# The first loads on two queues: ScalarE issues columns, constants and x, SyncE begins with the modulation weights

## The chip, the cores and the metric
One core of a Trainium2 chip. The time is that of one launch on the device, in microseconds (us), the median of several runs. The core has five engines that run their own instruction streams and meet at semaphores: TensorE (PE in the profile; PEld is its loading of weights), VectorE (DVE), ScalarE (ACT), GpSimd (POOL) and SyncE (SP), which here does nothing but issue loads and stores. The transfers themselves are done by 16 DMA engines that the core has for all its queues.

## The reference
Batch 1, 256 tokens, width 1024, everything in float32. A first block and then two layers of another kind:

```python
cond = silu(c)
mod = cond @ ada_w + ada_b                     # 1024 x 6144, split in sh1, sc1, g1, sh2, sc2, g2
h = rmsnorm(x, norm1_g) * (1 + sc1) + sh1
z = h @ w_in                                   # 1024 x 2048: xr, gr, u, v
y_lru = rg_lru(causal_conv(xr)) * gelu(gr)
y_sgu = spatial_gating(gelu(u), gelu(v))
x = x + g1 * (concat(y_lru, y_sgu) @ w_out)
h = rmsnorm(x, norm2_g) * (1 + sc2) + sh2
x = rmsnorm(x + g2 * moe(h), final_g)          # 4 groups of 8 experts, the top 2 of one group
for l in range(2):                             # attention, retention and mLSTM side by side
    x = hybrid_layer(x, ...)
return rmsnorm(x, final_norm_w_2)
```

The kernel computes all 32 experts, each for up to 64 tokens, so it reads every expert's three weights of 2 MB from HBM: 192 MB, and with the weights of the mixer and of the second block some 290 MB.

## The kernel before
The kernel is written engine by engine. What one engine does stands in functions that end in its name (mixer_pe, mixer_act, mixer_dve), and the order of the calls for an engine is the order of its instructions. Nothing plans or reorders it. All transfers are issued by SP.

Activations lie transposed: 128 channels by 256 tokens, eight such pieces for x (the tile xT, 128 x 2048, 1 MB). Weights come as one transfer per 2 MB piece of 1024 x 512 (16 KB in each of 128 partitions) into eight slots, six in the tile ring and two in the tile more; slot_of says which. The list stream gives their order: modulation weight 0, modulation weight 1, w_in piece 0, modulation weights 2 and 3, w_in piece 1, then the rest of the mixer, then six pieces for each pair of experts. Before SP loads a piece into a slot that has been used, it waits until the last reader has freed it (slot_free).

The beginning, step by step, with the lines as the profile names them:

- first_sp (L276 to L289) issues with no wait: cols (94 KB, all vectors as columns, c among them), the first constants (144 KB, the identity and the ones), x (1 MB), then the first six pieces of stream, with w_in piece 0 in two halves of 1 MB, the second of them behind modulation weight 3, and last four transfers that the gates and the router need. cols, the constants and x have semaphores of their own (s_cols, s_cst, s_x).
- ACT (L583 on) waits for cols and makes silu(c), waits for x and squares it in four instructions (L586), and takes the root of the mean squares (L589). The instruction before an activation that needs another function table is a table load.
- DVE copies silu(c) out to 32 columns (crep, L704), then makes 1/root (L708) and x/root (L712).
- PE sums the squares with a matrix of ones (stats, L395), and only then, since this is its order, does modulate_pe(0): silu(c) times modulation weight 0 (L338), summed into columns by turn_pe (L359) and DVE (L387, L389). Then modulation 1. With these, ACT makes the first half of hT, the normalized and modulated x (L600).
- PE goes on with the first half of w_in piece 0 on hT (xr, L425), between the parts of it modulations 2 and 3, and so on.

In the mixer, PE and DVE share the modulation weights 4 to 9 (DVE multiplies them row by row, L376 and L379). L541 are PE's last modulations before the router, at 120 to 126 us; they free slots for expert weights. The experts are L1042 and L1073 (up and down), the second block begins near 587 us.

Of the kernel before, what the change touches and what calls it, by code (L numbers as in the profile page):

```python
# [39 lines left out]
FEW = CONST["one"][0] + 32  # L40
# [18 lines left out]
def build(nc, p, out):  # L59
    pe, act, dve, pool, sp = nc.tensor, nc.scalar, nc.vector, nc.gpsimd, nc.sync  # L60
    with ExitStack() as ctx:
        def sb(name, *shape):
            return ctx.enter_context(nc.sbuf_tensor(name, [128, *shape], F32))

        def sem(name):
            return ctx.enter_context(nc.semaphore(name))
# [14 lines left out]
        xT = sb("xT", 8, T)  # L81
        cols = sb("cols", NCOLS)
        cst = sb("cst", EARLY)
# [108 lines left out]
        s_cols, s_x, s_cst, s_late, s_b1, s_out = (sem("s_" + n) for n in ("cols", "x", "cst", "late", "b1", "out"))  # L192
# [75 lines left out]
        def place(n):  # L268
            k, w = stream[n].shape[1], stream[n].shape[2]
            slot = ring[:, slot_of[n], :] if slot_of[n] < 6 else more[:, slot_of[n] - 6, :]  # L270
            return slot[:, 0:k * w].rearrange("p (k n) -> p k n", k=k)

        FIRST = 6

        def first_sp():
            sp.dma_start(cols[:, :], p["cols"]).then_inc(s_cols, 16)  # L276
            sp.dma_start(cst[:, 0:FEW], p["cst"][:, 0:FEW]).then_inc(s_cst, 16)
            sp.dma_start(xT[:, :, :], p["x"]).then_inc(s_x, 16)
            for n in range(FIRST):
                if n == W_IN[0]:  # L280
                    sp.dma_start(place(n)[:, 0:4, :], stream[n][:, 0:4, :]).then_inc(s_ring[slot_of[n]], 16)
                else:
                    sp.dma_start(place(n), stream[n]).then_inc(s_ring[slot_of[n]], 16)
                if n == ADA[3]:
                    sp.dma_start(place(W_IN[0])[:, 4:8, :], stream[W_IN[0]][:, 4:8, :]).then_inc(s_more[slot_of[W_IN[0]]], 16)
            sp.dma_start(cst[:, FEW:EARLY], p["cst"][:, FEW:EARLY]).then_inc(s_b1, 16)
            sp.dma_start(scr[:, 0:3072], p["b1"]).then_inc(s_b1, 16)
            sp.dma_start(rows[:, :], p["rows"]).then_inc(s_b1, 16)
            sp.dma_start(rw[:, :, :], p["rw"]).then_inc(s_b1, 16)  # L289
# [2190 lines left out]

        second_sp, second_pe, second_act, second_pool, second_dve, residual_act, residual_dve, again = second_block()
        first_sp()
        mixer_pe()
        mixer_act()
        mixer_dve()
# [145 lines left out]
```

## Time and profile before

| | us |
|---|---|
| median of 3 runs | 901.94 |
| lowest, highest | 900.82, 901.98 |
| the profiled execution | 900.98 |
| its span in the trace | 899.7 |

PE is busy for 855.5 us of the span (95%), DVE for 416.4, ACT for 302.0, POOL for 10.3. The transfers come to 292.96 MB, 326 GB/s over the span; SP's queue (q1) has its packets in work for 79.5% of the time of 16 engines. The rest of the packets are instruction fetches (q8 and q14). In the profile, 40 strips show equal slices of the span, 22.5 us each; the chain of waits goes back from the last instruction to what released each step. Durations in the trace are those of one execution.

### The profile page before, as it was taken

What the parts mean: (1) busy time and instruction counts of PE and PEld (TensorE: products, weight loads), DVE (VectorE), ACT (ScalarE), POOL (GpSimd) and SP (SyncE); (2) the same over time, 40 slices, a digit from 0 to 9 for tenths busy, and PEclk for the clock granted to TensorE, in tenths of its full rate; (3) what the DMA queues carried; (4) which work ended last, traced back from release to release, by engine and by line L of the source; (5) the groups of instructions that cost most, each with busy time, mean ns of one, the idle gap of its engine ahead of it and who ended that gap; (6) DMA issues with size and microseconds to landing.
All of it is one profiled execution on the core that took longest, in us unless ns stands there. A gap on an engine that the chain in (4) does not pass through costs nothing.

```text
span 899.7 us, 12205 instructions
## 1 busy us (share of the span) xinstructions
PE 855.5 (95%) x5030; PEld 554.2 (62%) x5030; DVE 416.4 (46%) x814; ACT 302.0 (34%) x548; POOL 10.3 (1%) x14
## 2 busy tenths in 40 slices
PE   5999999999998989899989899999999999999997
PEld 3668875344454334444444243489978999897985
DVE  3196964011210112001111011089898888989875
ACT  4253133111111111101111011174746666566663
POOL 0001000000000000000000000000100000010000
PEclk9999999999999999999999999999999999999999
DMA  9999989999999999999999999963425444653432
GB/s 371 424 428 427 402 351 428 410 428 428 427 429 428 426 428 427 428 426 428 428 428 427 428 422 423 402 245 123 168 86 187 142 164 180 180 154 105 179 141 71
DMA packets 34857, 292.96 MB, mean 326 GB/s; under 512 B 11376, under 2 KB 11888, under 8 KB 12912
## 3 DMA queue, kind: packets, MB, share of 16 engines
q1 hardware_dynamic: 34800, 292.16, 79.5%
q8 instruction: 41, 0.67, 0.3%
q14 instruction: 16, 0.13, 0.0%
HBM read 290.05 MB, written 1.05 MB: 324 GB/s over the span
## 4 chain that ended last, share of the span: by engine, by line
PE 71%; DMA 24%; DVE 3%; ACT 1%; SPq 1%; issue 1%; ACTq 0%
PE bank L1494 20%; PE bank L1042 16%; DMA more<-in_expert_w 14%; PE bank L1073 8%; DMA ring<-in_expert_w 7%; PE bank L1518 5%; PE bank L409 3%; DMA ring<-in_ada_w 3%; PE bank L1537 2%; PE bank L972 2%; DVE X L379 2%; PE bank L1013 2%; PE bank L452 2%; PE bank L425 1%; PE bank L1694 1%; PE bank L1720 1%
## 5 line engine op out<-in xcount | busy, mean ns | idle before, releaser
L1042 PE MATMUL bank<-ring,xg 128*64 128x512 f32 x760 | 234.5, 605 | 12.8 <-DMA ring<-in_expert_w 12.8
L1494 PE MATMUL bank<-HH,halves 128*128 128x256 f32 x848 | 164.0, 289 | 0.0
L1042 PEld LDWEIGHTS bank<-ring,xg 128*64 128x64 f32 x760 | 76.6, 139 | 123.1 <-issue 98.4
L1494 PEld LDWEIGHTS bank<-HH,halves 128*128 128x128 f32 x848 | 135.4, 192 | 4.6 <-issue 3.5
L1042 PE MATMUL bank<-more,xg 128*64 128x512 f32 x256 | 118.1, 614 | 7.5 <-DMA more<-in_expert_w 7.5
L1494 PE MATMUL bank<-HL,halves 128*128 128x256 f32 x424 | 120.3, 284 | 0.0
L1073 PE MATMUL bank<-ring,X 128*64 128x512 f32 x384 | 114.3, 595 | 0.7 <-ACT X L1113 0.7
L1160 DVE TENSOR_TENSOR X<-X,bank 128x512 f32<-128x512 f32 x16 | 11.0, 688 | 224.2 <-PE bank L1042 224.2
L1384 DVE TENSOR_TENSOR halves<-raw,halves 128x1024 fp32r<-128x1024 f32 (+1 forms) x84 | 91.9, 1128 | 6.4 <-ACT halves L1376 6.3
L1173 DVE SCALAR_TENSOR_TENSOR ygL<-bank,small,ygH 128x512 fp32r<-128x512 f32 x32 | 24.0, 750 | 136.2 <-ACT ygH L1120 136.2
L1494 PEld LDWEIGHTS bank<-HL,halves 128*128 128x128 f32 x424 | 81.6, 193 | 0.8 <-issue 0.5
L1376 ACT ACTIVATE halves<-raw 128x1024 fp32r<-128x1024 f32 (+1 forms) x84 | 78.2, 977 | 1.7 <-DMA raw<-in_units 1.7
L1042 PEld LDWEIGHTS bank<-more,xg 128*64 128x64 f32 x256 | 35.4, 141 | 51.9 <-issue 40.8
L1073 PEld LDWEIGHTS bank<-ring,X 128*64 128x64 f32 x384 | 35.2, 137 | 46.3 <-issue 43.4
L1120 ACT ACTIVATE ygH<-bank,small 128x512 fp32r<-128x512 f32 x32 | 22.0, 687 | 123.2 <-PE bank L1073 123.2
L1084 ACT ACTIVATE xg<-bank,modc 128x256 f32<-128x256 f32 x32 | 13.5, 472 | 138.0 <-PE bank L972 135.6
L1073 PE MATMUL bank<-more,X 128*64 128x512 f32 x128 | 56.6, 595 | 2.2 <-DMA more<-in_expert_w 1.5
L1101 ACT ACTIVATE X<-bank 128x512 f32<-128x512 f32 x16 | 9.6, 597 | 101.9 <-PE bank L1042 101.9
L1518 PE MATMUL bank<-halves,HH 128*128 128x512 f32 x128 | 41.8, 407 | 0.0
L1013 PE MATMUL bank<-PT,ygH 128*128 128x256 f32 x128 | 32.7, 293 | 0.4 <-DVE ygL L1173 0.4
L1073 PEld LDWEIGHTS bank<-more,X 128*64 128x64 f32 x128 | 16.9, 137 | 23.7 <-issue 20.0
L1013 PE MATMUL bank<-PT,ygL 128*128 128x256 f32 x128 | 31.1, 281 | 0.0
(369 smaller groups left out, 1217.9 us busy)
## 6 DMA issues: line engine op xcount, KB each, us to landing
ring<-in_expert_w SPq DMA_DIRECT2D x63, 2048.0 KB, 26.9
more<-in_expert_w SPq DMA_DIRECT2D x22, 2048.0 KB, 26.2
raw<-in_units SPq DMA_DIRECT2D x38, 1024.0 KB, 4.9
ring<-in_ada_w SPq DMA_DIRECT2D x10, 2048.0 KB, 20.9
ring<-in_expert_w SPq DMA_DIRECT2D x17, 1024.0 KB, 28.1
ring<-in_w_in SPq DMA_DIRECT2D x3, 2048.0 KB, 34.7
more<-in_ada_w SPq DMA_DIRECT2D x2, 2048.0 KB, 27.7
ring<-in_w_out SPq DMA_DIRECT2D x2, 2048.0 KB, 22.0
```

What stands on the lines that cost most here:

```text
L379: dve.scalar_tensor_tensor(a, w[:, k, :], cs[:, k:k + 1], a, ALU.mult, ALU.add).then_inc(s_fma, 1)
L409: t = pe.matmul(ps[:, T * j:T * j + T], w[:, k, 128 * (first + j):128 * (first + j) + 128], rhs[:, k, :], start=k == 0, stop=k == 7)
L452: t = pe.matmul(bank[6 + i][:, :], hT[:, k, 128 * i:128 * i + 128], w[:, k, :], start=k == 0, stop=k == 7)
L1013: t = pe.matmul(bank[ACC[a]][:, T * k:T * k + T], part(y[:, d:d + 128]), part(PT[n % 2][:, :]), start=n == 0 and k == 0 and j == 0, stop=n ...
L1042: t = pe.matmul(bank[3 + i][64 * x:64 * x + 64, :], xg[q % 2][:, k, o + 64 * x:o + 64 * x + 64], w[:, k, :], start=k == 0, stop=k == 7)
L1073: t = pe.matmul(bank[5 + a][64 * x:64 * x + 64, :], aT[:, f, 64 * x:64 * x + 64], place(at[x])[:, 4 * a + f, :], start=f == 0, stop=f == 3)
L1120: act.activation(part(ygH[:, 512 * a:512 * a + 512]), bank[5 + a][:, :], ACT.Copy, scale=weight[n % 2]).then_inc(s_ygh, 1)
L1173: dve.scalar_tensor_tensor(part(ygL[:, h]), bank[5 + a][:, :], weight[n % 2], ygH[:, h], ALU.mult, ALU.subtract).then_inc(s_ygl, 1)
L1376: act.activation(part(hi), src, ACT.Copy).then_inc(s_hi, 1)
L1384: dve.tensor_tensor(part(lo), src, hi, ALU.subtract).then_inc(s_lo, 1)
L1494: t = pe.matmul(ps[:, T * j:T * j + T], part(x[:, k, 128 * j:128 * j + 128]), part(y[:, k, :]), start=first and a == 0, stop=last and a == ...
L1518: t = pe.matmul(v3(ps[j][:, :], 2), part(x[:, k, 128 * j:128 * j + 128]), part(y), start=k == 0 and a == 0, stop=k == 7 and a == 2, skip_g ...
```

## The change
Three transfers go from the front of SP's queue to the front of ACT's. Both queues are then filled from the start of the kernel; the order within each is as before. Semaphores, tiles and readers are the same.

```diff
         FIRST = 6
 
+        def first_act():
+            act.dma_start(cols[:, :], p["cols"]).then_inc(s_cols, 16)
+            act.dma_start(cst[:, 0:FEW], p["cst"][:, 0:FEW]).then_inc(s_cst, 16)
+            act.dma_start(xT[:, :, :], p["x"]).then_inc(s_x, 16)
+
         def first_sp():
-            sp.dma_start(cols[:, :], p["cols"]).then_inc(s_cols, 16)
-            sp.dma_start(cst[:, 0:FEW], p["cst"][:, 0:FEW]).then_inc(s_cst, 16)
-            sp.dma_start(xT[:, :, :], p["x"]).then_inc(s_x, 16)
             for n in range(FIRST):
...
         first_sp()
+        first_act()
         mixer_pe()
         mixer_act()
         mixer_dve()
```

## Rows read from the trace of the kernel before

**Rows 1.** The page: its span, and the strips of TensorE's clock and of GB/s.
```profile
span 899.7 us, 12205 instructions
...
PEclk9999999999999999999999999999999999999999
...
GB/s 371 424 428 427 402 351 428 410 428 428 427 429 428 426 428 427 428 426 428 428 428 427 428 422 423 402 245 123 168 86 187 142 164 180 180 154 105 179 141 71
```

**Rows 2.** The chain of waits: start us, us, what; ahead of them its shares to 110 us.
```profile
by line: PE bank L409 25.1%; DMA ring<-in_ada_w 23.6%; PE bank L452 12.5%; DVE X L379 9.7%; PE bank L425 8.4%; PE bank L466 3.1%; issue 2.6%; PE bank L338 1.7%; PE bank L359 1.6%; DVE xT L796 1.6%; DVE yT L783 1.6%; DVE modc L387 1.3%; SPq 
...
4.50 25.92 DMA ring<-in_ada_w
...
30.55 1.92 PE bank L338 x16
...
247.72 28.63 DMA more<-in_expert_w
```

**Rows 3.** Timeline to 31 us: start us, us, engine, line, operation, what it waited for.
```profile
0.74 1.28 ACT L583 ACT_TABLE_LOAD   x1 [0.74 <-PEq L2623]
...
7.12 2.19 ACT L586 ACTIVATE yT<-xT 128x512 f32<-128x512 f32 x4 [4.23 <-DMA xT<-in_x]
...
7.89 6.23 PE L395 MATMUL bank<-yT,cst 128*128 128x256 f32 x16 [7.89 <-ACT yT L586]
9.32 1.28 ACT L589 ACT_TABLE_LOAD   x1
...
14.05 1.92 PE L338 MATMUL bank<-ring,crep 128*32 128x512 f32 x16
...
21.96 2.08 PE L425 MATMUL bank<-hT,ring 128*128 128x256 f32 x8 [1.39 <-ACT hT L600]
...
24.40 1.92 PE L338 MATMUL bank<-ring,crep 128*32 128x512 f32 x16 [0.36 <-DMA ring<-in_ada_w]
...
28.52 1.89 PE L425 MATMUL bank<-hT,ring 128*128 128x256 f32 x8
```

**Rows 4.** Timeline of SyncE's queue: when it issues, and for how long.
```profile
0.74 0.39 SPq L276 DMA_DIRECT2D cols<-in_cols  x1
...
1.65 0.43 SPq L278 DMA_DIRECT2D xT<-in_x  x1
2.13 0.91 SPq L283 DMA_DIRECT2D ring<-in_ada_w  x2
```

**Rows 5.** Windows at the start; last columns granted clock, DMA share, GB/s.
```profile
1.00:5.00 4.00, 0.00 (x0) 0.00 (x0) 1.42 (x11) 1.23 (x2) 0.00 (x0) 1.00 0.77 200
2.00:3.00 1.00, 0.00 (x0) 0.00 (x0) 0.17 (x1) 0.23 (x2) 0.00 (x0) 1.00 1.41 279
```

**Rows 6.** DMA queues (packets, MB, share of 16 engines), 240 to 244, then 710 to 714.
```profile
q1 hardware_dynamic: 109, 1.69, 99.7%
q8 instruction: 1, 0.02, 1.7%
...
q1 hardware_dynamic: 43, 0.22, 13.3%
q8 instruction: 1, 0.02, 1.9%
```

**Rows 7.** DMA issues to 36 us: count, KB each, us from issue to landing.
```profile
ring<-in_ada_w SPq DMA_DIRECT2D x6, 2048.0 KB, 23.1
...
xT<-in_x SPq DMA_DIRECT2D x1, 1024.0 KB, 5.4
...
cst<-in_cst SPq DMA_DIRECT2D x1, 144.0 KB, 2.4
cols<-in_cols SPq DMA_DIRECT2D x1, 94.0 KB, 1.9
```

**Rows 8.** Windows 123 to 126 us; then SyncE's waits from 120 to 130.
```profile
123.00:126.00 3.00, 3.00 (x19) 2.76 (x19) 0.00 (x0) 0.00 (x0) 0.00 (x0) 1.00 0.26 109
...
SPq L302 <- PE bank L541: 10.3, 1, 10.3
```

## The prediction

> **What bounds the kernel now.** I read the strip of the whole span first. From the second slice up to about 585 us the DMA engines move 402 to 429 GB/s, with one sag to 351 in the sixth [rows 1]. So the stream of weights is near its limit, and the question is whether it or TensorE (PE) ends last at the beginning, where the change is. The next view for that is the chain of waits. The chain starts with the issues of SyncE's queue (SP) and then lies on one long DMA piece, from 4.50 to 30.42, which is the fourth modulation weight on its way; PE starts on it at 30.55 [rows 2]. Of the chain's first 110 us DMA has 23.6%, which is this one piece; from there on it is PE and VectorE (DVE) up to 126 us [rows 2].
>
> The timeline of the first 31 us says that this DMA wins by a hair. PE finished the matmuls before that weight at 28.52 + 1.89 = 30.41, and the weight was there at 30.42 [rows 2, 3]. So there are two chains of equal length. The first is the DMA stream. The second starts with x: x lands, ScalarE (ACT) squares it from 7.12, PE sums the squares with ones (7.89 to 14.12), then in PE's order come the first and the second modulation, the first matmuls on hT (end 24.04), the third modulation (starts 24.40, after 0.36 us of waiting for its weight), and the fourth at 30.55 [rows 3]. The readers of x have no slack but that 0.36 us and the 0.01 us at the end. PE can't take the modulations first: the sums of squares stand ahead of them in its queue.
>
> **What the change does to the stream.** SP loses three issues: its first modulation weight was issued at 2.13 and now at 0.74, 1.39 us earlier [rows 4]. What is that worth to the stream? Between 1 and 5 us it moved 4 us x 200 GB/s = 0.80 MB, where a full queue moves about 0.42 MB per us (1.69 MB in 4 us) [rows 5, 6]. With the big rows there from about 1.9 us, the stream would be (5.0 - 1.9) - 0.80/0.42 = 1.2 us ahead. The fourth weight could land at 30.42 - 1.2 = 29.2 (29.0 by the full 1.39), since the bytes that land before it are at most the same.
>
> ACT gains three issues, 0.39 to 0.43 us each by SP's own rows [rows 4]: 1.3 us of its queue. Behind them wait its first table load, 1.28 us at 0.74 [rows 3], the activation of c, and the squares. Table load and c then end near 2.1 + 1.28 + 0.2 = 3.6. PE wants c, which DVE has copied out for it by then, only at 14.05 [rows 3], and the squares wait for x until 7.1 anyway. I cost these issues at nothing; were the cover gone it would be 1.3 us. An issue by ACT isn't in this trace: 0.4 us by the nearest row, up to 1 us each as a bound, and even then c is done by 5.5 us.
>
> **What it does to x.** This decides. Before, cols, the first constants and x went down one queue in front of everything. They landed 1.9, 2.4 and 5.4 us after issue: x at 1.65 + 5.4 = 7.05 [rows 4, 7]. Now they are in one queue and the weights in another, and both are open from 0.74 us. Both use the same 16 engines: one queue alone takes 99.7% of them when it is full [rows 6], so x can't keep its place unless its queue is preferred.
>
> How do two queues share? The only second traffic in the trace is that of the instruction queue q8. One 16 KB packet of it, in 4 us with the other queue at 99.7% of the engines, took 1.7% of 16 x 4 us = 1.09 us; in 4 us with the other queue at 13.3% it took 1.9%, 1.22 us [rows 6]. A packet isn't served slower beside a full queue, so the engines look like they take packet by packet, not slices of two packets at once. If they take them in turn, every row of the ACT queue costs one row of the SP queue. Each of the 128-partition transfers gives each engine 128/16 = 8 rows, however short: cols 8, constants 8, x 8, and against these stand the first modulation weight 8, the second 8, and the first half of w_in 8. So x is complete when these six are: 94 + 144 + 1024 + 2048 + 2048 + 1024 = 6382 KB = 6.54 MB (sizes in [rows 7] and in the diff's order of loads; a whole weight is 2048 KB).
>
> The pace of landing, from this trace: the third modulation weight came at 24.4 [rows 3], and with it 94 + 144 + 1024 + 3 x 2048 + 1024 = 8430 KB = 8.63 MB; 0.80 of it was moved by 5.0 us, so 7.83 MB in 19.4 us, 404 GB/s. Then x lands at 1.9 + 6.54/0.404 = 18.1 us, 11 us later than before. The squares start at 18.2.
>
> From there by the rows as they are: 24.04 - 7.12 = 16.92 us until PE is ready for the third modulation, 30.55 - 24.40 = 6.15 more to the fourth, so 18.2 + 16.92 + 6.15 = 41.3 against 30.55: **+10.7 us**. The slack of 0.36 is used up in it, and the stream's gain is worth nothing, its weights lying ready. In the 16.92 is PE's start from rest: 16 matmul records took 6.23 us, 0.39 us each, which is also the length of a later one of this shape (8 in 1.89, 0.24 apart) at the other pace [rows 3]. The granted clock is at 9 tenths or more throughout [rows 1], so nothing was throttled; the slow ones look like the lower of TensorE's two levels, 1.2 for 2.4 GHz. PE has rested before x in both kernels; I keep 6.23, with 16 x 0.24 = 3.8 as the lower bound (-2.4 us).
>
> **Is it given back later?** The weights would be ahead, so a late PE could catch up only where it waited for DMA. It doesn't between 30.55 and 126 us. Between 123 and 126 us the DMA engines are at 0.26 of their share, because SP's next load waits 10.3 us for a slot that PE's L541 frees [rows 8]: there the stream follows PE, and a late PE makes it as late. From there to 560 us the chain goes back and forth between slots that PE frees and loads that take 28.6 us [rows 2] to land. Both are tied to that point, so all of the 10.7 us arrives at the end. The most that could come back is that sag, 0.74 x 3 = 2.2 us of idle engines; but a stream with more loaded can't use it, since slots are what it lacks, and I take nothing back. The other loads of the beginning (block constants, wanted only after 57 us) keep their place and come earlier.
>
> **Sum.** Own time of the profiled execution 900.98 (span 899.7 [rows 1], 1.3 around it) + 10.7 = 911.7. That execution is 0.96 under the median of 901.94; on the median it is 912.6. The measurement tells 0.2%, 1.8 us, from no change.
>
> **Rivals.**
> The engines take a transfer's whole share of rows as one turn. If cols is first, x is behind two weights but ahead of the half w_in: 5.49 MB, 1.9 + 13.6 = 15.5, which gives +8.1: 910.0. If the weight is first it's the sum above. For it: nothing in the trace tells a row from a group of rows. The Trainium skill (DMA: Bandwidth & Descriptors, Queues, rings and completion order) says that an engine goes round its queues and drains a packet of typically 9 to 17 descriptors before it changes; by that rule this rival holds, since 8 rows and a completion are nine. The q8 rows agree with turns and can't show their size. The same page (Issuing engines are not separate DMA queues) speaks against the change: issuing from several engines saves only issue time.
>
> The engines share by bytes. Then x's queue gets a half: 1.29 MB at 0.21 MB per us, x at 8.1 to 8.4, the squares 1.0 to 1.3 later, less 0.36 of slack: +0.7 to +1.0, 902.8. If the short rows slip through but x's 8 KB rows alternate with 16 KB rows, x gets a third: from 3.0 us 3.1 MB at 0.404, x at 10.8, +3.4: 905.3. For it: in 2 to 3 us the engine share reads 1.41 [rows 5], so short packets do overlap. Against it: the q8 rows.
>
> Not slower: x is not held up, because its queue is served first or the weights' first rows come after it. The place is the start of the squares; the price is that of the earlier weights. The 0.36 us of waiting before the third modulation goes, and with it that much; for the full 1.39 the squares would have to start at 7.12 + 0.36 - 1.39 = 6.1. The point from which it decides is x at 7.4 (7.12 + 0.36, less the 0.07 from landing to start): below it the change gains, above it each us of x costs one. That gives 901.6. Against it: cols, constants and x alone took until 7.05 with the engines to themselves.
>
> The change doesn't do quite what it says: ACT's table load stands ahead of its issues, and all three go 1.28 us later. x is then behind 1.3 us more of weights: 913.9. Against it: the load at 9.32 followed directly on the squares, placed at its own activation, so I expect the first one behind the issues.
>
> **Numbers.** Turns of rows 0.46 (912.6), turns of whole shares 0.15 (910.0), by bytes or by a third 0.24 (902.8 to 905.3), not held up 0.10 (901.6), later issues 0.05 (913.9). The likeliest gives 912.6. The range goes from 902.6, which leaves only the case of 901.6 below, to 914.2, above the late issues. Slower by over 0.2%: 0.46 + 0.15 + 0.05 + about half of the 0.24 = 0.77. Same: the other half, and most of the not held up, 0.20. Faster: 0.03, for something that I don't see, since the whole 1.39 us is under the bound.
>
> **What would show it.** Right: the squares (L586) start at 18.2 and wait for the DMA of x, the sums of squares end near 25, the fourth modulation starts at 41, no wait of PE for a modulation weight, and the same offset at 126 us and at the end. cols lands near 7 us and the constants near 12. Wrong if x lands before 11 us; wrong in another way if x is late and the offset shrinks between 30 and 600 us.

## The result, and the profile after

| us | before | changed |
|---|---|---|
| median (4 runs each) | 901.59 | 913.12 |
| lowest, highest | 900.82, 901.98 | 912.82, 913.96 |
| profiled execution, its span | 900.98, 899.7 | 912.88, 911.6 |

The changed kernel is slower: ratio 1.0124, 95% interval 1.0112 to 1.0136, or 11.5 us by the medians. The forecast was 912.6 (+10.7, on the 901.94 known then), with turns of rows as the likeliest case.

The timeline of the first 43 us (start us, us, engine, line, operation, what it waited for) is what to read first. Line numbers from first_sp on are two higher than before.

```profile
0.74 0.40 ACTq L276 DMA_DIRECT2D cols<-in_cols  x1
0.74 0.86 SPq L285 DMA_DIRECT2D ring<-in_ada_w  x2
...
1.67 0.45 ACTq L278 DMA_DIRECT2D xT<-in_x  x1
...
2.15 1.28 ACT L585 ACT_TABLE_LOAD   x1 [2.15 <-issue]
...
8.99 0.21 ACT L585 ACTIVATE small<-cols 128x8 f32<-128x8 f32 x1 [5.56 <-DMA cols<-in_cols]
...
14.42 1.26 DVE L706 TENSOR_SCALAR crep<-cst,small 128x32 f32<-128x32 f32 x8 [5.26 <-DMA cst<-in_cst]
...
19.31 2.19 ACT L588 ACTIVATE yT<-xT 128x512 f32<-128x512 f32 x4 [10.11 <-DMA xT<-in_x]
...
20.08 5.34 PE L397 MATMUL bank<-yT,cst 128*128 128x256 f32 x16 [20.08 <-ACT yT L588]
...
25.35 1.92 PE L340 MATMUL bank<-ring,crep 128*32 128x512 f32 x16
...
33.26 3.36 PE L427 MATMUL bank<-hT,ring 128*128 128x256 f32 x8 [1.38 <-ACT hT L602]
...
36.55 2.16 PE L340 MATMUL bank<-ring,crep 128*32 128x512 f32 x16
...
42.73 1.92 PE L340 MATMUL bank<-ring,crep 128*32 128x512 f32 x16
```

They answer to [rows 3, 4]. The weights are issued at 0.74, as meant. The squares start at 19.31 instead of 7.12, after 10.11 us of waiting for x, and everything on PE is behind them: the first modulation at 25.35 (14.05), the third at 36.55 (24.40), the fourth at 42.73 (30.55). No wait of PE for a weight is left. The first table load stands behind ACT's three issues, not ahead of them, so the case of later issues (913.9) didn't happen.

The chain of waits (start us, us, what) has x where it had the fourth weight [rows 2]:

```profile
1.67 17.62 DMA xT<-in_x
20.08 5.34 PE bank L397 x16
```

The DMA issues to 36 us answer to [rows 7] (count, KB each, us from issue to landing): 17.6 us for 5.4 (x), 13.1 for 2.4 (the constants), 8.2 for 1.9 (cols).

```profile
xT<-in_x ACTq DMA_DIRECT2D x1, 1024.0 KB, 17.6
...
cst<-in_cst ACTq DMA_DIRECT2D x1, 144.0 KB, 13.1
cols<-in_cols ACTq DMA_DIRECT2D x1, 94.0 KB, 8.2
```

How the engines divide themselves is seen in the DMA queues of single windows (packets, MB, share of 16 engines; q1 is SP's queue, q10 ACT's). First 1 to 3 us, then all up to 4 us, then 4 to 5, 10 to 11, and 14 to 18:

```profile
q1 hardware_dynamic: 16, 0.26, 60.5%
...
q1 hardware_dynamic: 32, 0.52, 46.0%
q10 hardware_dynamic: 16, 0.01, 4.0%
...
q1 hardware_dynamic: 27, 0.44, 103.8%
q10 hardware_dynamic: 29, 0.02, 6.4%
...
q1 hardware_dynamic: 27, 0.44, 103.1%
q10 hardware_dynamic: 26, 0.03, 8.3%
...
q10 hardware_dynamic: 104, 0.85, 51.1%
q1 hardware_dynamic: 104, 0.85, 50.9%
```

One packet here, one there, whatever their size. Up to 3 us there are 16 packets of the first weight, as many as there are engines, and none of cols, although both were issued at 0.74. By 4 us there are 32 and 16. From 4 to 5 and from 10 to 11 us SP's 27 packets of 16 KB carry 0.44 MB and ACT's 26 to 29 short ones 0.02 or 0.03. From 14 us x's rows of 8 KB meet the half w_in's rows of 8 KB, 104 to 104, and only there are the bytes equal.

Further on, the window of 3 us from 135 and SP's waits from 120 to 145 us (windows: last columns granted clock, DMA share, GB/s) answer to [rows 8]:

```profile
135.00:138.00 3.00, 3.00 (x20) 2.76 (x20) 0.00 (x0) 0.00 (x0) 0.00 (x0) 1.00 0.33 137
...
SPq L304 <- PE bank L543: 10.3, 1, 10.3
```

The same sag, 12 us later, with the same wait of 10.3 us. SP's load behind it goes out at 138.41 instead of 126.25, an offset of 12.16, and the span ends with 11.9: nothing to speak of was given back.

### The profile page after: what moved, and what is told of

It is laid out like the page before. It is cut to its first block, busy times and chain, and to the rows that moved or that the text cites. A ratio compares the mean times of both kernels' runs of the same rounds, so it can differ in the third digit from the quotient of the medians.

```text
span 911.6 us, 12205 instructions
## 1 busy us (share of the span) xinstructions
PE 853.9 (94%) x5030; PEld 548.8 (60%) x5030; DVE 416.2 (46%) x814; ACT 301.7 (33%) x548; POOL 10.3 (1%) x14
## 3 DMA queue, kind: packets, MB, share of 16 engines
q10 hardware_dynamic: 432, 1.29, 0.4%
## 4 chain that ended last, share of the span: by engine, by line
PE 72%; DMA 22%; DVE 3%; ACT 1%; issue 1%; SPq 0%; ACTq 0%
PE bank L1496 20%; PE bank L1044 16%; DMA more<-in_expert_w 14%; PE bank L1075 8%; DMA ring<-in_expert_w 7%; PE bank L1520 5%; PE bank L411 3%; PE bank L1539 2%; DMA xT<-in_x 2%; PE bank L974 2%; PE bank L427 2%; DVE X L381 2%; PE bank L1015 2%; PE bank L454 2%; PE bank L340 1%; PE bank L1696 1%
## 5 line engine op out<-in xcount | busy, mean ns | idle before, releaser
L1044 PEld LDWEIGHTS bank<-ring,xg 128*64 128x64 f32 x760 | 72.1, 140 | 126.4 <-issue 103.6
## 6 DMA issues: line engine op xcount, KB each, us to landing
ring<-in_w_out SPq DMA_DIRECT2D x2, 2048.0 KB, 10.7
```

The costliest lines, as they stand in the source:

```text
L1044: t = pe.matmul(bank[3 + i][64 * x:64 * x + 64, :], xg[q % 2][:, k, o + 64 * x:o + 64 * x + 64], w[:, k, :], start=k == 0, stop=k == 7)
```

## The experiments

Theory T: each DMA engine takes one row (one packet) of each queue in turn, so a short row of ACT's queue costs one row of SP's; x is late for that reason alone, and PE carries the delay to the end. The rivals were a share by bytes or time, turns of whole transfers, and a queue of ACT that is slow of itself. Each kernel's trace is of one execution; "fourth modulation" is its start there. Ratios are to the kernel before, run on the same chip, with 95% intervals.

| kernel | median us | ratio (interval) | x landed | fourth modulation |
|---|---|---|---|---|
| sp_waits_x | 905.88 | 1.0036 (1.0021 to 1.0052) | 6.7 | 33.64 |
| halves | 907.78 | 1.0065 (1.0042 to 1.0088) | 14.3 | 36.94 |
| quarters | 904.87 | 1.0028 (1.0015 to 1.0040) | 10.6 | 33.91 |
| x_on_act | 900.99 | 0.9992 (0.9979 to 1.0006) | 5.8 | 30.17 |
| small_on_act | 904.98 | 1.0036 (1.0025 to 1.0047) | 5.9 | 34.63 |
| x_first | 914.04 | 1.0135 (1.0120 to 1.0151) | 11.5 | 42.97 |
| warm_after | 912.36 | 1.0117 (1.0097 to 1.0137) | 19.3 | 42.80 |
| warm35_after | 912.83 | 1.0129 (1.0109 to 1.0150) | 19.2 | 41.02 |
| warm_before | 901.74 | 1.0000 (0.9991 to 1.0010) | 6.8 | 32.35 |
| x_act_warm | 900.00 | 0.9977 (0.9962 to 0.9992) | 5.8 | 29.47 |

"x landed" is issue plus time to landing, or the start of the squares where ACT waited for nothing else. The medians of before were 902.28 for sp_waits_x, halves, quarters and x_on_act, 901.78 for the next four kernels that ran together (small_on_act, x_first, warm_after, x_act_warm), and 901.62 for the other two.

**Is ACT's queue slow of itself? (sp_waits_x)**

```diff
         def first_sp():
+            sp.wait_ge(s_x, 16)
             for n in range(FIRST):
```

> The changed kernel, but SP waits for x before its first weight, so ACT's three loads have the engines to themselves. If only the weights beside them made them late, x lands at 7.05 as before and PE's stats start at 7.9; the weights are issued at 7.1 instead of 2.13 and lose what the engines could have moved until about 8.5, so the third and fourth modulation come 2 to 2.5 us later than before: 903.6 to 904.1. If ACT's queue is slow of itself, x lands at 8.4 or later and the time is 905 or more.

In its timeline x is there at 6.75, a little earlier than in the kernel before [rows 3], and the first modulation is what waits now:

```profile
6.75 2.19 ACT L589 ACTIVATE yT<-xT 128x512 f32<-128x512 f32 x4 [3.14 <-DMA xT<-in_x]
...
14.60 1.92 PE L341 MATMUL bank<-ring,crep 128*32 128x512 f32 x16 [1.56 <-DMA ring<-in_ada_w]
```

So three loads on ACT's queue are as quick as on SP's when nothing runs beside them. What made them late is the weights. The time, 0.36% or 3.2 us over before (3.6 by the medians), is above the 2 to 2.5 that I had reckoned and in the range that I had given to a slow queue, but x's landing rules that rival out. About 1.5 us of it are PE's: its first hT matmuls took 3.07 us for 2.08, and the third modulation 2.45 for 1.92.

**Is it the size of SP's rows? (halves and quarters)** Same bytes, same order; only the rows of the first two weights are shorter. The lines are those of quarters; halves has range(2) and slices of four. In both, PE waits for all parts of a weight (not shown).

```diff
                 if n == W_IN[0]:
...
+                elif n < 2:
+                    for q in range(4):
+                        h = slice(2 * q, 2 * q + 2)
+                        sp.dma_start(place(n)[:, h, :], stream[n][:, h, :]).then_inc((s_aside, s_sooner)[n] if q < 3 else s_ring[slot_of[n]], 16)
                 else:
```

> The changed kernel, with modulation weights 0 and 1 issued in two transfers each, so that SP's first 32 rows per engine are 8 KB instead of 16. Same bytes in the same order. Turns of rows: x is complete after 3 MB of weights instead of 5 MB, so it lands 2.10 MB / 0.404 = 5.2 us earlier than 19.3, at 14.1, and the kernel takes 908. Sharing by bytes or by time: x lands at 19 as in the changed kernel, 913.

> The same with four transfers each, rows of 4 KB. Turns of rows: cols, constants and x meet three quarters of weight 0, 1.57 MB; x lands at 3.1 + (1.29 + 1.57)/0.404 = 10.2, 3.1 us later than before the change, and the kernel takes 901.6 + 3.1 - 0.36 = 904.3. By bytes or time: 913 as in the changed kernel.

x's landing in the DMA issues, halves first and then quarters:

```profile
xT<-in_x ACTq DMA_DIRECT2D x1, 1024.0 KB, 12.6
...
xT<-in_x ACTq DMA_DIRECT2D x1, 1024.0 KB, 8.9
```

With rows of 16, 8 and 4 KB in the first two weights, x landed at 19.3, 14.3 and 10.6; expected were 14.1 and 10.2. The times, 907.8 and 904.9, follow (908 and 904.3 expected). A share by bytes or by time, which would have left x at 19, is out. This alone doesn't part rows from whole transfers, since each half and quarter is a transfer too; the windows above do.

**Does the number of rows in ACT's queue count, and not their bytes? (small_on_act and x_first)**

The lines are those of small_on_act, where ACT issues cols and the first constants alone. In x_first nothing moves to SP: the line of x goes ahead of ACT's other two.

```diff
         def first_act():
...
-            act.dma_start(xT[:, :, :], p["x"]).then_inc(s_x, 16)
 
         def first_sp():
+            sp.dma_start(xT[:, :, :], p["x"]).then_inc(s_x, 16)
```

> ACT issues cols and the first constants, SP x and then the weights. Only 238 KB stand in ACT's queue. Turns of rows: the 8 rows of cols meet x's 8 rows and land near 5 us; the 8 rows of the constants (144 KB) meet weight 0 and land about 5 us later, near 10.1. PE's stats need them and start at 10.2 instead of 7.89; less the 0.36 of slack the kernel is 1.9 us slower than before. If short transfers slip through and only x's size was the trouble, the constants land by 4, x at 5.5, and it is not slower than before.

> The changed kernel with x ahead of cols and the constants in ACT's queue. Turns of rows: x's rows meet weight 0, so x lands at 3.1 + (1.05 + 2.10)/0.404 = 10.9 instead of 19.3; cols meet weight 1 and land near 16.3; the constants meet the half of w_in and land near 19.3. PE's stats need the constants and start there, 0.7 us earlier than in the changed kernel: 912.4. If x's landing itself set the time, the kernel would be 8 us faster than the changed one.

In small_on_act x was ready for the squares at 6.28, and PE stood until 11.51 for 144 KB of constants:

```profile
6.28 2.17 ACT L588 ACTIVATE yT<-xT 128x512 f32<-128x512 f32 x4
...
11.51 5.80 PE L397 MATMUL bank<-yT,cst 128*128 128x256 f32 x16 [11.51 <-DMA cst<-in_cst]
```

The constants landed 10.3 us after their issue, 1.4 later than expected, and the kernel was 0.36% slower (3.2 us; 1.9 expected). Short transfers don't slip through. The sums began 3.6 us later than before and the fourth modulation was 4.1 later, for on the way the first hT matmuls took 2.96 us (2.08 before) and the third modulation 2.57 (1.92). In x_first x landed at 11.5, cols at 16.7, the constants at 19.7 (10.9, 16.3 and 19.3 expected), and PE began the sums at 19.67 on the constants. Its 914.0 lies near the changed kernel's 913.1, not 8 us under it: whichever transfer is last in ACT's queue pays for all rows ahead of it. The 0.7 us gain over the changed kernel that I expected did not show: PE began the sums 0.41 us earlier, and they took 5.93 us for 5.34.

**The same rule used the other way (x_on_act).** ACT issues x alone, and SP cols and constants ahead of the weights, so that x's 8 rows meet short ones.

```diff
         def first_act():
-            act.dma_start(cols[:, :], p["cols"]).then_inc(s_cols, 16)
-            act.dma_start(cst[:, 0:FEW], p["cst"][:, 0:FEW]).then_inc(s_cst, 16)
             act.dma_start(xT[:, :, :], p["x"]).then_inc(s_x, 16)
         def first_sp():
+            sp.dma_start(cols[:, :], p["cols"]).then_inc(s_cols, 16)
+            sp.dma_start(cst[:, 0:FEW], p["cst"][:, 0:FEW]).then_inc(s_cst, 16)
```

> ACT issues x alone at 0.74; SP issues cols, the first constants, then the weights, the first weight at 1.65. If the engines take one row from each queue in turn, x's 8 rows per engine meet the 8 short rows of cols, and x lands at about 5.1 us (7.05 before); the weights are issued 0.48 us earlier than before. PE then waits for the weights alone, the fourth modulation starts at 29.6 to 29.9 (30.55), and the whole is 0.6 to 0.9 us faster than before: 900.8. Rival: a load issued by ACT comes late of itself, whatever lies beside it (the first packets of its queue in the changed kernel were seen only after 3 us). Then x lands at 7 or later and the time is that of before or above it.

x landed 5.1 us after its issue, at 5.8 (about 5.1 expected), and the fourth modulation started 0.38 us earlier than before, at 30.17 (29.6 to 29.9 expected). The short rows paid for it: cols took 4.4 us to land for 1.9, the constants 5.1 for 2.4. The median is 900.99; the interval of the ratio holds 1, so this is no measurable gain. Why so little came of 1.2 us of earlier x is in its timeline: the first modulation ended sooner, PE waited for the second weight, and then went slowly.

```profile
6.61 5.36 PE L397 MATMUL bank<-yT,cst 128*128 128x256 f32 x16 [6.61 <-ACT yT L588]
...
16.29 3.18 PE L340 MATMUL bank<-ring,crep 128*32 128x512 f32 x16 [1.09 <-DMA ring<-in_ada_w]
```

From 16 to 19 us its granted clock was 0.64.

**PE's pace (warm_after, warm35_after, warm_before, x_act_warm).** These add matmuls of a zeroed tile into an unused bank ahead of the sums of squares: 32, 35, 9, and for x_act_warm 6 there and 2 behind the first modulation. They compute nothing that is used.

```diff
+            pe.wait_ge(s_fill, 1)
+            for _ in range(32):
+                pe.matmul(bank[7][:, 0:T], Pm0[:, 0, 0:128], Pm0[:, 1, :], start=True, stop=True)
             pe.wait_ge(s_cst, 16)
```

> The changed kernel, with 32 extra matmuls of zeros on PE ahead of the sums of squares, into a bank that is not in use, while PE waits for x. If the slow matmuls are PE's start from rest, the stats take 16 x 0.24 = 3.8 us instead of 5.34, the first hT matmuls 2.1 instead of 3.36, and the kernel is 1.5 to 2.8 us faster than the changed one: 910.3 to 911.6. If the slow stretches come from something else, both stay and it takes 913.

> warm_after with 35 extra matmuls instead of 32: they should end at 19.6 instead of 18.2, 0.5 us before the stats instead of 1.95. If that gap is what let PE fall back, the stats now take 3.7 us instead of 5.4 and the kernel is 1.7 us faster than the changed one, near 911.4; if the slow stretch at the first hT matmuls goes too, 910.2. If the gap is not the reason, the stats still take 5.3 us.

warm_after first, then warm35_after:

```profile
20.11 5.38 PE L397 MATMUL bank<-yT,cst 128*128 128x256 f32 x16 [1.95 <-ACT yT L591]
...
33.33 3.00 PE L430 MATMUL bank<-hT,ring 128*128 128x256 f32 x8 [1.38 <-ACT hT L605]
```
```profile
20.00 3.69 PE L397 MATMUL bank<-yT,cst 128*128 128x256 f32 x16 [0.16 <-ACT yT L591]
...
31.53 3.62 PE L430 MATMUL bank<-hT,ring 128*128 128x256 f32 x8 [1.38 <-ACT hT L605]
```

With 1.95 us of rest before them the sums went at the slow pace all the same (granted clock 0.57 from 20 to 24 us), and warm_after's 912.36 missed the 910.3 to 911.6 that I had expected. With 0.16 us of rest they took 3.69 (1.00). The two kernels differ only in three matmuls, that is, in the rest, and in warm35_after the fourth modulation came 1.7 us earlier than in the changed kernel. But the slow stretch at the first hT matmuls stayed in both, and the median of warm35_after, 912.83, can't be told from the changed kernel's 913.12; I had expected about 911.4. In its trace SP's load behind L543 still goes out 1.70 us earlier than in the changed kernel (136.71 for 138.41), and the span ends only 0.1 us earlier: the gain is lost later.

> The kernel before the change with 9 extra matmuls ahead of the stats, nothing else. The stats take 3.7 us instead of 6.23, but weights 2 and 3 land when they did (24.4 and 30.4), so the fourth modulation starts at 30.5 and the time is that of before within 0.3 us. If it is 1.5 us faster, then the gain of x_act_warm was PE's pace alone and had nothing to do with the queues.

> x_on_act with 6 such matmuls ahead of the stats and 2 behind the first modulation. x_on_act had the weights earlier but its second modulation took 3.18 us for 1.92 elsewhere. If PE's pace is the reason, the second modulation ends 1.26 us earlier, the fourth starts at about 29.2 instead of 30.17, and the kernel is 1.3 us faster than before the change: 900.6. If the weights are what it waits for, the fourth modulation stays at 30.2 and the time at that of x_on_act.

warm_before took 901.74, no change, as expected, but not in the way that I expected: its fourth modulation was at 32.35, not 30.5. The sums went down to 3.62 us, PE then waited 1.58 us for the second weight, and its second modulation took 3.49 us and the first hT matmuls 3.41. So the fourth modulation was 1.8 us later than before, and the median shows nothing of it. x_act_warm is the only one that is faster than the kernel before: 900.00, ratio 0.9977 (0.9962 to 0.9992), some 2 us, with 900.6 expected. The sums and the second modulation run at full pace, PE waits for the third weight, and the fourth modulation is at 29.47 (29.2 expected):

```profile
6.62 3.69 PE L397 MATMUL bank<-yT,cst 128*128 128x256 f32 x16 [0.26 <-ACT yT L593]
...
16.05 1.92 PE L340 MATMUL bank<-ring,crep 128*32 128x512 f32 x16 [0.73 <-DMA ring<-in_ada_w]
...
23.53 1.92 PE L340 MATMUL bank<-ring,crep 128*32 128x512 f32 x16 [0.71 <-DMA ring<-in_ada_w]
```

x_on_act and warm_before, each with one part of it, can't be told from before. But the intervals of x_on_act and x_act_warm overlap, and warm_before lacks the two matmuls behind the first modulation, so it isn't shown that the gain needs both parts. The fourth modulation accounts for 1.1 of the 2 us.

## Why the prediction was right

**The stream's start** came 1.39 us earlier and was worth nothing, since no weight was waited for after it.

**ACT's issues** cost nothing: 0.40 to 0.46 us each where 0.39 to 0.43 was assumed, and the table load behind them ended at 3.4, long before cols landed at 9.0.

**x's landing** was the step that decides: 19.3 instead of 7.05, with 18.1 predicted. The mechanism, a row for a row, is shown twice: by nearly equal packet counts in each microsecond, and by row size (16, 8, 4 KB give 19.3, 14.3, 10.6). The size was 1.2 us short, and cols (9.0 for about 7) and the constants (14.3 for about 12) were late in the same way. The bytes did flow as reckoned: the DMA queues up to 18.0 us, and then up to 19.3, show

```profile
q1 hardware_dynamic: 416, 5.24, 71.8%
q10 hardware_dynamic: 408, 1.23, 17.7%
...
q1 hardware_dynamic: 464, 5.77, 73.4%
q10 hardware_dynamic: 432, 1.29, 17.4%
```

By 18.0 us 6.47 MB had gone, where I put 6.54 by 18.1. But 24 of ACT's 432 packets were still to come, and when x was seen to land 7.06 MB had gone. I took x as complete as soon as the bytes up to it are through; the 0.52 MB that SP's queue moved beyond that are the missing 1.2 us. The kernel before shows such a lag too: 1.29 MB stand in the queue up to the end of x, and 1.73 MB had gone by 7.0 us, when it landed. The evidence from the instruction queue in [rows 6] pointed the right way; it couldn't show the size of a turn.

**Turns of whole transfers** would let the 8 short rows of one transfer through together, 128 packets over the 16 engines in a burst. In the windows of one microsecond between 4 and 12 us q10 has 21 to 37 packets in each and never a burst, and by 4 us, with 32 packets of the first weight gone, ACT's first 16 had gone too. Here the turn is one row of up to 16 KB. The Trainium skill (DMA: Bandwidth & Descriptors, Queues, rings and completion order) gives an engine's turn as a packet of typically 9 to 17 descriptors. This trace doesn't agree: as the profile counts them, q10's 432 packets for three transfers of 128 rows are 9 on each engine for each transfer, and by 4 us the engines had changed queues after one.

The Trainium skill also says (DMA: Bandwidth & Descriptors, Issuing engines are not separate DMA queues) that issuing from several engines saves only issue time. Here 1.39 us of issue were saved and worth nothing, and the three transfers took 6.3 to 12.2 us longer to land: it can cost.

**From x to the fourth modulation** I took 16.92 + 6.15 us. The sums took 5.34 us for 6.23 (0.89 less) and the first hT matmuls 3.36 for 2.08 (1.28 more). With the 1.1 us of x this makes 41.3 - 0.89 + 1.28 + 1.1 = 42.8; measured were 42.73. That the first two nearly cancel is luck: from rest the sums took 5.3 to 6.7 us in the kernels without extra matmuls, and I can't say what sets it. The 1.28 has its row in the windows of the changed kernel (the third number from the end is the granted clock, the mean of the window):

```profile
33.00:36.00 3.00, 2.74 (x8) 2.18 (x8) 2.37 (x15) 1.59 (x4) 0.00 (x0) 0.61 0.97 402
```

In the kernel before, the granted clock was 1.00 from 21.9 to 24.4 us, where the same matmuls ran. I had said that nothing was throttled, from the strip of the whole span in [rows 1]; a slice of 22.5 us that reads 9 tenths can hide 5 us at 0.6. And 1.00 is no proof of the fast pace: it stands at every window from 8 to 14 us of the kernel before, where the sums went at 0.39 us each.

**Nothing given back**: the offset was 12.16 at 138 us and 11.9 at the end. Across the kernels the offset of the fourth modulation and that of the median go together only within some 2 us:

| | fourth modulation, offset | median, offset |
|---|---|---|
| changed | +12.2 | +11.5 |
| halves | +6.4 | +5.5 |
| small_on_act | +4.1 | +3.2 |
| quarters | +3.4 | +2.6 |
| sp_waits_x | +3.1 | +3.6 |
| warm_before | +1.8 | +0.1 |
| x_on_act | -0.4 | -1.3 |
| x_act_warm | -1.1 | -1.8 |
| x_first | +12.4 | +12.3 |
| warm_after | +12.2 | +10.6 |
| warm35_after | +10.5 | +11.2 |

That PE's delay is carried through is shown for several microseconds, not for one or two. One reason for the scatter is in the traces: the stretch after 126 us, where loads and PE release each other, isn't always equally long. From SP's issue at that point to the end of the span it took 773.4 us before, 772.3 in warm_before (from 128.03), 772.4 in x_on_act (from 125.85) and 775.5 in sp_waits_x (from 129.31). Why is open. Whether the slow stretches of PE also fall otherwise in executions that weren't profiled, no trace here can show.

**The sum**: +10.7 predicted, +11.5 measured by the medians and +11.9 by the profiled executions. The path and the mechanism were as predicted; the difference is x's landing and the two terms of PE.

## What to carry to other kernels

A second issuing queue isn't a second lane. If SP's and ACT's queues are both full, a transfer waits, besides for its own queue's bytes, for as many rows of the other queue as there are rows up to its end in its own. Put small, urgent transfers in front of the bulk in the same queue, as the kernel before does. A large urgent one beside short rows lands earlier (5.8 for 7.05 us here), but the short ones then land later, and that alone gained no time that could be measured. Before moving issues to save a microsecond, find which transfer the first instruction of the long chain waits for, and what would be served beside it.

## What I had not expected of the hardware

- Of two queues issued at the same moment (0.74 us), the one with the 16 KB rows was served first, with 16 packets; the other's first packet came after 3 us.
- 144 KB of constants took 10.3 us (small_on_act), 13.1 (changed) and 18.0 (x_first) to land beside the weights, by what stood ahead of them in ACT's queue, and 2.4 us in the kernel before.
- PE falls to the lower of its two levels (1.2 for 2.4 GHz) within its work, not only at the start, and the granted clock shows this only in windows of a few us: 0.61 from 33 to 36 us of the changed kernel, 0.64 from 16 to 19 us of x_on_act after 1.09 us of waiting, 0.57 from 20 to 24 us of warm_after, which had rested 1.95 us after 16.7 us of work. Each such stretch cost 1.3 to 1.7 us. What decides where they fall in the changed kernel's hT matmuls, with gaps equal to those before, stays open.
